# Rounding the weight slabs beside attention in quarters, between the units of the softmax

## The chip, the cores and the metric

The kernel runs on one core of one Trainium2 chip. The metric is the device time of one execution in microseconds; the median of three runs stands for a kernel. Besides TensorE (matmuls), a core has VectorE, ScalarE and GpSimd, each with its own instruction stream that is worked off in order, and SyncE, which here only starts DMAs. The engines meet through semaphores.

## What is computed

A decoder trunk of two layers over 272 positions (16 learned ones and 256 tokens) of width 1024, in float32. Layer 0 is sliding-window attention with 16 heads, 4 of keys and values, a sink for each head and a relative-position bias, followed by a dense SwiGLU. Layer 1 is RWKV-7 time mixing followed by a mixture of 8 experts, two for each token. After each of the four parts stands a layer norm of the weighted residual. The change lies beside attention:

```
qkv = einsum('bld,de->ble', x, w_qkv) + b_qkv
s_band = where(ok_band, q . k_band + bias_band, NEG_INF)      # and s_meta
m = max(max(s_band), max(s_meta), sink)
p_band = exp(s_band - m);  p_meta = exp(s_meta - m)
denom = sum(p_band) + sum(p_meta) + exp(sink - m)
o = (p_band . v_band + p_meta . v_meta) / denom
y = einsum('ble,ed->bld', o, w_o)
h = layer_norm(ALPHA * h + y)
```

## The kernel before

All large weights come as 395 slabs of 128x2048 float32 (1 MB). SyncE loads them in order into a ring of 7 slots, `ring`; from slab 7 on each load waits until the slab that had the slot has been split (`slab_taken`). A product is made from three: each operand is written as a rounded high half and a low half that is the rest, and high times high, high times low and low times high are added. For a slab, ScalarE writes the high half `w_hi` (`round_slab`, L1068 to L1073, the page's L1073), VectorE writes `w_lo` = `ring` - `w_hi` (`split_slab`, through the helper `tt` of L1364). Both have two buffers, slab n in n % 2. ScalarE may round slab n when the high half of slab n-2 has been used (`hi_free`) and slab n-2 has been split; VectorE may split it when slab n-2 has been multiplied (`slab_used`).

Slab 0 holds the key weights, 1 the values, 2 to 5 the queries (`SL_Q` = 2, two blocks of 128 queries each), 6 to 9 W_o (`SL_WO` = 6). The slabs that the change touches are 4, 5, 6 and 7.

Attention is cut into 24 units, a unit being one of three blocks of positions (96, 96 and 80 queries against 96, 192 and 224 keys) and two heads. They come in four periods of six, `s, r = divmod(u, 6)`; period s works on query blocks 2s and 2s+1, which slab 2+s gives. Each engine runs its own loop over u, written by hand:

- TensorE: `scores(u + 2)` (L611), which waits for the bias step of unit u+1; while s < 3 and r < 4 a fourth of the products of the next query slab (L593, L594, L599); `transposes(u - 1)` of the probabilities (L624); on even u the product of probabilities and values (L640).
- VectorE: waits for the exponentials of unit u, normalises it (L1447, L1449), then `biased(u + 2)`, which is the bias step (L1424, out of the PSUM banks of the scores, so that TensorE may write the next ones) and the minimum for the softmax (L1427); on even u the low half of an output block, `o_lo`; at r == 4 `split_slab(SL_Q + 2 + s)`.
- ScalarE: the exponentials of unit u+1 (L1121), the copy of the transposed probabilities of unit u-2 (L1138), on odd u the high half of an output block (L1129), at r == 3 the copy of the new queries (`keep_queries`, L1114), and at r == 4 `round_slab(SL_Q + 2 + s)`.

So at the fifth unit of every period one slab is rounded whole and split whole. Slabs 4 and 5 are multiplied in the next period, slabs 6 and 7 in the product with W_o behind the last unit. SyncE and GpSimd have nothing in the loop over units. Behind it come W_o, the layer norm, the dense layer and the rest, each on the result of the one before.

Of the kernel before, what the change touches and what calls it, by code (L numbers as in the profile page):

```python
# [20 lines left out]
F32, I32 = mybir.dt.float32, mybir.dt.int32  # L21
F32R = mybir.dt.float32r
ACT = mybir.ActivationFunctionType
# [17 lines left out]
SLOTS = 7  # L41
SL_K, SL_V, SL_Q, SL_WO = 0, 1, 2, 6
# [95 lines left out]
GROUP = 512  # L138
# [19 lines left out]
def build(nc, A, OUT):  # L158
    ctx = ExitStack()
    with ctx:  # L160
# [3 lines left out]
        def sem(name):  # L164
            return ctx.enter_context(nc.semaphore(name))

        ring = sb("ring", [P, SLOTS, TILES * P])
# [37 lines left out]
        to_head = carve(len(MASKS) * CH, KC, HEADS, memory=spare)  # L205
        from_head = carve(len(MASKS) * CH + KC * HEADS, KC, P, memory=spare)[0:HEADS]

        def columns_of(l):
            return slice(N_META if l == 3 else 0, T)

# [89 lines left out]
        w_hi = sb("w_hi", [P, 2, TILES * P], F32R)  # L300
        w_lo = sb("w_lo", [P, 2, TILES * P], F32R)
# [32 lines left out]
        loaded = [sem(f"slab_loaded{j}") for j in range(SLOTS)]  # L334


        hi_set, slab_taken = sem("slab_rounded"), sem("slab_split")
        hi_free, slab_used = sem("rounded_weights_used"), sem("slab_multiplied")
        h_hi_set, h_split = sem("h_rounded"), sem("h_split")
        dense_sig, dense_gate, gu_free = sem("dense_sigmoid"), sem("dense_gate"), sem("dense_hidden")  # L340
        dense_hi, dense_split = sem("dense_hidden_rounded"), sem("dense_hidden_split")
# [725 lines left out]
        def _(act):  # L1067
            def round_slab(n):  # L1068
                act.wait_ge(loaded[n % SLOTS], 16 * (n // SLOTS + 1))
                if n >= 2:  # L1070
                    act.wait_ge(hi_free, n - 1)
                    act.wait_ge(slab_taken, n - 1)
                act.activation(w_hi[:, n % 2, :], ring[:, n % SLOTS, :], ACT.Copy).then_inc(hi_set, 1)  # L1073

            def layer_norm(l):
                cols = columns_of(l)
                for k in range(KC):
                    act.wait_ge(ln_dve[l], k + 1)
                    act.activation(sq[:, k, cols], z[:, k, cols], ACT.Square).then_inc(ln_act[l], 1)
                act.wait_ge(ln_dve[l], 9)  # L1080
                act.activation(rstd[:, cols], rstd[:, cols], ACT.Sqrt).then_inc(ln_act[l], 1)
                for k in range(KC):
                    act.wait_ge(ln_dve[l], 11 + k)
                    act.activation(h[:, k, cols], z[:, k, cols], ACT.Identity, bias=v_of(f"b{l}", k))\  # L1084
                       .then_inc(ln_act[l], 1)
                    if l == 0:
                        act.activation(h_hi[:, k, :], z[:, k, :], ACT.Identity, bias=v_of(f"b{l}", k))\
                           .then_inc(h_hi_set, 1)
# [17 lines left out]
            for t in range(3):  # L1106
                n = min(P, T - P * t)
# [35 lines left out]
            for u in range(len(UNITS)):  # L1143
                s, r = divmod(u, 6)
                if u + 1 < len(UNITS):
                    exps(u + 1)
                if u >= 2:
                    keep_transposed(u - 2)
                if u >= 5 and u % 2:
                    keep_out((u - 5) // 2)  # L1150
                if s < 3 and r == 3:
                    keep_queries(s + 1)
                if r == 4:
                    round_slab(SL_Q + 2 + s)
            keep_transposed(len(UNITS) - 2)
            keep_transposed(len(UNITS) - 1)
            keep_out(len(UNITS) // 2 - 2)
# [41 lines left out]
            for j in range(12):  # L1199
                n = SL_RKV + j  # L1200
# [36 lines left out]
            for part, c, *level in order:  # L1237
                n, q = tokens_of(c), c % 2
# [110 lines left out]
        def _(dve):  # L1349
# [16 lines left out]
            def split_slab(n):  # L1366
                dve.wait_ge(hi_set, n + 1)
                if n >= 2:
                    dve.wait_ge(slab_used, n - 1)
                tt(w_lo[:, n % 2, :], ring[:, n % SLOTS, :], w_hi[:, n % 2, :].bitcast(F32), ALU.subtract)\  # L1370
                    .then_inc(slab_taken, 1)

            def left(lo, x, hi, wait, value, done):

                dve.wait_ge(wait, value)
                tt(lo, x, hi.bitcast(F32), ALU.subtract).then_inc(done, 1)
# [64 lines left out]
            for u, (t, m) in enumerate(UNITS):  # L1441
                s, r = divmod(u, 6)
                q0, qn, kn = Q_TILES[t]
                dve.wait_ge(sc_exp, u + 1)
                if u:
                    dve.wait_ge(sc_norm, u)
                nr.step(dve.reciprocal(rden[0:qn, :], den[0:qn, u % 4, :]))  # L1447
                for p in range(2):
                    i = dve.tensor_scalar(pr[0:qn, u % 4, p, 1:kn + 1], pr[0:qn, u % 4, p, 1:kn + 1],  # L1449
                                          rden[0:qn, p:p + 1], None, ALU.mult)  # L1450
                i.then_inc(sc_norm, 1)
                if u + 2 < len(UNITS):
                    biased(u + 2)
                if u >= 6 and u % 2 == 0:
                    split_out(u // 2 - 3)
                if r == 4:
                    split_slab(SL_Q + 2 + s)
            split_out(len(UNITS) // 2 - 3)
            split_out(len(UNITS) // 2 - 2)
            split_out(len(UNITS) // 2 - 1)  # L1460
# [24 lines left out]
            s = Steps(xx_steps)  # L1485
# [475 lines left out]
```

## Time and profile before

| | |
|---|---|
| median of 3 runs | 1764.15 us (1762.57 to 1768.33) |
| the profiled execution | 1763.99 us, of which the span of instructions is 1762.2 us |
| TensorE matmul busy | 1649.7 us (94%) |
| VectorE busy | 1295.3 us (74%) |
| ScalarE busy | 1000.0 us (57%) |
| the units of attention | about 38 to 121 us |
| mean granted TensorE clock | 0.955 of full speed |

The shares are means over stages with different limits. The experts take over half of the time; attention is 83 us of it. A timeline row gives start, duration, engine, line, operation, output and inputs, the count of merged instructions, and in brackets the idle time before it with what ended it. Instructions overlap a little at their ends, so the distance between two starts is the better price of an instruction in a row. In a row of windows the granted clock (PEclk) is 1.00 at the upper of TensorE's two levels, 2.4 GHz, and 0.50 at the lower, 1.2 GHz. The tile `arena` holds queries, scores and probabilities alike; its rows are told apart by their lines.

### The profile page before, as it was taken

The page shows a single profiled execution, that of the slowest core. Times are in us where ns is not written, and L with a number is a line of the kernel's source. Part 1 is how long each engine was busy: PE and PEld are TensorE (multiplying, and loading weights), DVE is VectorE, ACT ScalarE, POOL GpSimd, SP SyncE. Part 2 cuts the span into 40 slices and gives each one's busy share as a digit, 9 for nine tenths or more (in the row PEclk, how much of TensorE's full clock was granted, in tenths as well). Part 3 has the DMA queues.
Part 4 walks back from the last instruction along what each step waited for, and adds up shares of the span by engine and source line. Part 5 has one row for each costly group of instructions (what it writes and reads, how often), then busy time and mean ns, then how long its engine had stood idle before and what let it go on. Part 6 is the DMA issues. An engine that isn't in the chain of part 4 may idle for free.

```text
span 1762.2 us, 29867 instructions
## 1 busy us (share of the span) xinstructions
PE 1649.7 (94%) x12114; PEld 1297.7 (74%) x12114; DVE 1295.3 (74%) x1256; ACT 1000.0 (57%) x1027; POOL 72.8 (4%) x111
## 2 busy tenths in 40 slices
PE   7778999989999996799999999999999999999995
PEld 6557999967889974777777777777777777777774
DVE  3655554465755425579899899898998998998984
ACT  3544443334802212367777777777777777777773
POOL 3000000000035300000000000000000000000000
PEclk9869999989989986899999999999999999999997
DMA  9412544621400001249999999999999999999980
GB/s 262 169 49 102 183 168 167 226 101 51 166 26 4 4 3 48 103 150 374 368 358 371 372 354 372 369 358 370 359 369 372 357 369 370 359 371 366 361 330 26
DMA packets 60292, 425.42 MB, mean 241 GB/s; under 512 B 6887, under 2 KB 8023, under 8 KB 9224
## 3 DMA queue, kind: packets, MB, share of 16 engines
q1 hardware_dynamic: 58152, 416.52, 62.6%
q0 software_dynamic: 2016, 7.13, 1.6%
q8 instruction: 91, 1.49, 0.3%
q14 instruction: 33, 0.27, 0.0%
HBM read 422.28 MB, written 1.12 MB: 240 GB/s over the span
## 4 chain that ended last, share of the span: by engine, by line
PE 71%; DVE 3%; ACT 2%; issue 1%; ACTq 0%; POOL 0%; DVEq 0%
PE PS L512 53%; PE PS L798 6%; PE PS L513 5%; PE PS L1012 1%; PE PS L814 1%; DVE arena L1364 1%; PE PS L968 1%; PE PS L823 1%; PE PS L552 1%; PE PS L998 0%; PE PS L999 0%; PE PS L558 0%; PE PS L936 0%; PE PS L776 0%; ACT h L1084 0%
## 5 line engine op out<-in xcount | busy, mean ns | idle before, releaser
L1364 DVE TENSOR_TENSOR w_lo<-ring,w_hi 128x2048 fp32r<-128x2048 f32 x395 | 903.3, 2288 | 208.9 <-ACT w_hi L1293 88.5
L1293 ACT ACTIVATE w_hi<-ring 128x2048 fp32r<-128x2048 f32 x336 | 644.7, 1919 | 264.3 <-PE PS L512 241.7
L512 PE MATMUL PS<-w_hi,x_hi 128*96 128x512 f32 x896 | 353.9, 395 | 0.7 <-ACT x_hi L1285 0.7
L512 PE MATMUL PS<-w_hi,x_lo 128*96 128x512 f32 x896 | 352.5, 393 | 0.0
L512 PE MATMUL PS<-w_lo,x_hi 128*96 128x512 f32 x896 | 243.0, 392 | 0.0
L1073 ACT ACTIVATE w_hi<-ring 128x2048 fp32r<-128x2048 f32 x59 | 112.9, 1914 | 168.2 <-issue 89.3
L512 PEld LDWEIGHTS PS<-w_lo,x_hi 128*96 128x96 f32 x896 | 144.6, 161 | 62.1
L512 PEld LDWEIGHTS PS<-w_hi,x_lo 128*96 128x96 f32 x896 | 144.8, 162 | 58.2
L512 PEld LDWEIGHTS PS<-w_hi,x_hi 128*96 128x96 f32 x896 | 144.6, 161 | 58.1 <-ACT x_hi L1285 1.0
L512 PE MATMUL PS<-w_hi,hid_hi 128*96 128x512 f32 x448 | 176.7, 394 | 0.0
L512 PE MATMUL PS<-w_hi,hid_lo 128*96 128x512 f32 x448 | 176.0, 393 | 0.0
L512 PE MATMUL PS<-w_lo,hid_hi 128*96 128x512 f32 x448 | 121.9, 394 | 0.0
L798 PE MATMUL PS<-arena 64*64 64x64 f32 (+6 forms) x3360 | 110.9, 218 | 5.6 <-DVE arena L1364 2.3
L798 PEld LDWEIGHTS PS<-arena 64*64 64x64 f32 (+3 forms) x3360 | 102.3, 131 | 13.8 <-issue 9.6
L1258 ACT ACTIVATE arena<-PS 128x256 f32<-128x256 f32 (+2 forms) x84 | 32.3, 389 | 141.2 <-PE PS L798 88.0
L1364 DVE TENSOR_TENSOR arena<-arena,PS 128x272 f32<-128x272 f32 (+6 forms) x102 | 54.4, 535 | 60.2 <-PE PS L798 56.5
L513 PE MATMUL PS<-h_hi,w_hi 128*128 128x272 f32 x352 | 91.2, 293 | 6.8 <-DVE h_lo L1364 6.7
L512 PEld LDWEIGHTS PS<-w_lo,hid_hi 128*96 128x96 f32 x448 | 72.2, 161 | 31.7
L512 PEld LDWEIGHTS PS<-w_hi,hid_hi 128*96 128x96 f32 x448 | 72.2, 161 | 30.8
L512 PEld LDWEIGHTS PS<-w_hi,hid_lo 128*96 128x96 f32 x448 | 72.3, 161 | 30.7
L513 PE MATMUL PS<-h_lo,w_hi 128*128 128x272 f32 x352 | 90.7, 291 | 0.0
L1364 DVE TENSOR_TENSOR experts<-experts,PS 96x512 f32<-96x512 f32 (+1 forms) x113 | 76.0, 672 | 0.0
(258 smaller groups left out, 2035.8 us busy)
## 6 DMA issues: line engine op xcount, KB each, us to landing
ring<-in_slabs SPq DMA_DIRECT2D x395, 1024.0 KB, 4.9
arena<-in_lora POOLq DMA_DIRECT2D x1, 1152.0 KB, 5.4
h<-in_h SPq DMA_DIRECT2D x1, 1088.0 KB, 6.6
arena<-bias_lines POOLq DMA_DIRECT2D x1, 1056.0 KB, 19.9
arena<-bias_lines POOLq DMA_DIRECT2D x1, 1040.0 KB, 24.6
arena<-in_lora POOLq DMA_DIRECT2D x1, 1024.0 KB, 12.0
out<-h SPq DMA_DIRECT2D x1, 1024.0 KB, 4.7
arena<-in_lora POOLq DMA_DIRECT2D x1, 512.0 KB, 6.5
```

Source lines behind the costliest of these rows:

```text
L512: return pe.matmul(out, x, w, start=start, stop=stop) if tokens_stay else \
L513: pe.matmul(out, w, x, start=start, stop=stop)
L552: mm = pe.matmul(PS[:, 0, cols], ones_d[:, :], z[:, k, cols], start=k == 0, stop=k == KC - 1)
L798: mm = pe.matmul(PS[64 * p:64 * p + n_out, b + g, at:at + width], lhsT(m, p), rhs(m, p), start=i == 0, stop=i == len(pairs) - 1)
L814: mm = pe.matmul(out[64 * p:64 * p + n, :, 0:n], by_feature(x, c)(m, p), r_kk[64 * p:64 * p + 64, :, T * m + CH * c:T * m + CH * c + n], s ...
L823: mm = pe.matmul(PS[64 * p:64 * p + n, b + g, col + CH * (m % 4):col + CH * (m % 4 + 1)], x(m, p), masks[64 * p:64 * p + 64, MASKS.index(" ...
L968: mm = pe.matmul(PS[:, 2 * (j % 4) + i, 0:HALF], rows[:, t, P * k:P * k + P], pick[:, t, 4 * half:4 * half + 4, :].rearrange("p e c -> p ( ...
L1012: mm = pe.transpose(PS[:, 4 + g % 2, CAP * j:CAP * (j + 1)], hid_rows[0:CAP, g % 2, P * j:P * (j + 1)], eye[0:CAP, 0:CAP])
L1073: act.activation(w_hi[:, n % 2, :], ring[:, n % SLOTS, :], ACT.Copy).then_inc(hi_set, 1)
L1258: act.activation(out, rows, ACT.Copy).then_inc(c_act, 1)
L1293: act.activation(w_hi[:, n % 2, :], ring[:, n % SLOTS, :], ACT.Copy).then_inc(hi_set, 1)
L1364: tt = lambda o, a, b, op=ALU.mult: dve.tensor_tensor(out=o, in0=a, in1=b, op=op)
```

## The change

The rounding and the split of slabs 4 to 7 are each done in four parts of 512 columns. ScalarE does quarter r behind its work of unit r of the period, r = 0 to 3, instead of the whole at r = 4. VectorE does quarter r - 1 behind its work of unit r, r = 1 to 4. The conditions that the whole rounding waited for stand before quarter 0 (and are asked for four units earlier), the one of the split before VectorE's quarter 0. Two new semaphores count the first three quarters; the last quarter of each kind counts `hi_set` and `slab_taken` as the whole did, so TensorE's and SyncE's conditions are unchanged. `GROUP` is 512.

```diff
+        def quarter(x, i):
+            return x[:, GROUP * i:GROUP * (i + 1)]
...
+        part_hi, part_lo = sem("slab_quarters_rounded"), sem("slab_quarters_split")
...
+            def round_quarter(n, i):
+                if i == 0:
+                    act.wait_ge(loaded[n % SLOTS], 16 * (n // SLOTS + 1))
+                    act.wait_ge(hi_free, n - 1)
+                    act.wait_ge(slab_taken, n - 1)
+                act.activation(quarter(w_hi[:, n % 2, :], i), quarter(ring[:, n % SLOTS, :], i), ACT.Copy)\
+                   .then_inc(hi_set if i == 3 else part_hi, 1)
...
                 if s < 3 and r == 3:
                     keep_queries(s + 1)
-                if r == 4:
-                    round_slab(SL_Q + 2 + s)
+                if r < 4:
+                    round_quarter(SL_Q + 2 + s, r)
...
+            def split_quarter(n, i):
+                if i == 3:
+                    dve.wait_ge(hi_set, n + 1)
+                else:
+                    dve.wait_ge(part_hi, 3 * (n - SL_Q - 2) + i + 1)
+                if i == 0:
+                    dve.wait_ge(slab_used, n - 1)
+                tt(quarter(w_lo[:, n % 2, :], i), quarter(ring[:, n % SLOTS, :], i),
+                   quarter(w_hi[:, n % 2, :].bitcast(F32), i), ALU.subtract)\
+                    .then_inc(slab_taken if i == 3 else part_lo, 1)
...
-                if r == 4:
-                    split_slab(SL_Q + 2 + s)
+                if 1 <= r < 5:
+                    split_quarter(SL_Q + 2 + s, r - 1)
```

The first place is VectorE in the second period, from the minimum of unit 11 over the bias step of unit 12 to that of unit 13 (both L1424, 96x2x97). Before:

```order
L1427 TENSOR_REDUCE arena<-arena 80x2
L1447 RECIPROCAL arena<-arena 80x2
L1449 TENSOR_SCALAR arena<-arena 80x224 x2
L1424 SCALAR_TENSOR_TENSOR arena<-PS,arena 96x2x97
L1427 TENSOR_REDUCE arena<-arena 96x2
L1364 TENSOR_TENSOR o_lo<-PS,o_hi 128x2x80
L1364 TENSOR_TENSOR w_lo<-ring,w_hi 128x2048
L1447 RECIPROCAL arena<-arena 80x2
L1449 TENSOR_SCALAR arena<-arena 80x224 x2
L1424 SCALAR_TENSOR_TENSOR arena<-PS,arena 96x2x97
```

The same stretch of VectorE in the changed kernel, whose lines are 12 to 23 higher:

```order
L1450 TENSOR_REDUCE arena<-arena 80x2
L1376 TENSOR_TENSOR w_lo<-ring,w_hi 128x512
L1470 RECIPROCAL arena<-arena 80x2
L1472 TENSOR_SCALAR arena<-arena 80x224 x2
L1447 SCALAR_TENSOR_TENSOR arena<-PS,arena 96x2x97
L1450 TENSOR_REDUCE arena<-arena 96x2
L1376 TENSOR_TENSOR o_lo<-PS,o_hi 128x2x80
L1376 TENSOR_TENSOR w_lo<-ring,w_hi 128x512
L1470 RECIPROCAL arena<-arena 80x2
L1472 TENSOR_SCALAR arena<-arena 80x224 x2
L1447 SCALAR_TENSOR_TENSOR arena<-PS,arena 96x2x97
```

The whole w_lo ahead of the bias step of unit 13 has become one of 128x512; another of them now stands ahead of the bias step of unit 12, and two more before this piece.

The second place is ScalarE at the turn from unit 9 to unit 10: the copies of the queries (L1114), the exponentials of unit 11 (L1121, 80x225), the transposed probabilities (L1138), and then, before:

```order
L1129 ACTIVATE o_hi<-PS 128x2x80
L1114 ACTIVATE arena<-PS,vec 128x272 x2
L1121 ACTIVATE arena<-arena 80x225 x2
L1138 ACTIVATE arena<-PS 128x2x96
L1138 ACTIVATE arena<-PS 64x2x96
L1073 ACTIVATE w_hi<-ring 128x2048
L1121 ACTIVATE arena<-arena 96x97 x2
```

And the same stretch of ScalarE in the changed kernel:

```order
L1141 ACTIVATE o_hi<-PS 128x2x80
L1126 ACTIVATE arena<-PS,vec 128x272 x2
L1084 ACTIVATE w_hi<-ring 128x512
L1133 ACTIVATE arena<-arena 80x225 x2
L1150 ACTIVATE arena<-PS 128x2x96
L1150 ACTIVATE arena<-PS 64x2x96
L1133 ACTIVATE arena<-arena 96x97 x2
```

The fourth quarter of w_hi stands behind the queries and ahead of the exponentials of unit 11; nothing stands any more between the transposed probabilities and the exponentials of unit 12.

## Rows read from the trace of the kernel before

**Rows 1.** TensorE's waits, 36 to 122 us: total us, times, longest us.

```profile
PE PS L611 <- DVE arena L1424: 14.6, 6, 4.4
```

**Rows 2.** Busy us by window, with TensorE's granted clock (PEclk).

```profile
core 0: us, PE busy (x) PEld busy (x) DVE busy (x) ACT busy (x) POOL busy (x), PEclk, DMA share, GB/s
40.00:42.00 2.00, 1.46 (x7) 0.96 (x7) 1.61 (x6) 1.55 (x8) 0.00 (x0) 0.64 1.01 188
...
78.00:80.00 2.00, 0.02 (x2) 0.05 (x2) 1.93 (x6) 0.00 (x0) 0.00 (x0) 0.52 0.00 0
...
108.00:110.00 2.00, 2.00 (x13) 0.94 (x10) 1.42 (x6) 1.44 (x6) 0.00 (x0) 0.50 0.02 4
...
124.00:126.00 2.00, 2.00 (x11) 2.00 (x10) 0.00 (x0) 0.00 (x0) 0.00 (x0) 0.53 0.00 0
```

**Rows 3.** Timeline of VectorE, bias step of unit 12 to that of unit 13.

```profile
73.92 0.36 DVE L1424 SCALAR_TENSOR_TENSOR arena<-PS,arena 96x194 f32<-96x194 f32 x1 [1.11 <-PE PS L611]
...
74.58 0.31 DVE L1364 TENSOR_TENSOR o_lo<-PS,o_hi 128x160 fp32r<-128x160 f32 x1
76.59 2.29 DVE L1364 TENSOR_TENSOR w_lo<-ring,w_hi 128x2048 fp32r<-128x2048 f32 x1 [1.70 <-ACT w_hi L1073]
78.80 0.15 DVE L1447 RECIPROCAL arena<-arena 80x2 f32<-80x2 f32 x1
...
79.49 0.35 DVE L1424 SCALAR_TENSOR_TENSOR arena<-PS,arena 96x194 f32<-96x194 f32 x1
```

**Rows 4.** Timeline of ScalarE at 74.65 us.

```profile
74.65 1.91 ACT L1073 ACTIVATE w_hi<-ring 128x2048 fp32r<-128x2048 f32 x1
```

**Rows 5.** Timeline of TensorE, the score products (L611) of four units.

```profile
67.09 0.61 PE L611 MATMUL PS<-arena 64*80 64x225 f32 x4
...
70.19 0.61 PE L611 MATMUL PS<-arena 64*80 64x225 f32 x4
...
79.98 0.96 PE L611 MATMUL PS<-arena 64*96 64x193 f32 x4 [4.38 <-DVE arena L1424]
...
85.59 0.57 PE L611 MATMUL PS<-arena 64*96 64x193 f32 x4
```

**Rows 6.** Timeline of VectorE, the bias steps (L1424) of units 10 and 11.

```profile
67.75 0.62 DVE L1424 SCALAR_TENSOR_TENSOR arena<-PS,arena 80x450 f32<-80x450 f32 x1 [0.60 <-PE PS L611]
...
70.85 0.62 DVE L1424 SCALAR_TENSOR_TENSOR arena<-PS,arena 80x450 f32<-80x450 f32 x1 [0.91 <-PE PS L611]
```

**Rows 7.** Groups by form, 0 to 700 us: count, busy us, mean ns, idle.

```profile
L1073 ACT ACTIVATE w_hi<-ring 128x2048 fp32r<-128x2048 f32 x57 | 109.1, 1914 | 159.7 <-issue 89.3 <-PE PS L513 68.9 <-DMA ring<-in_slabs 1.5
...
L1258 ACT ACTIVATE arena<-PS 128x512 f32<-128x512 f32 x8 | 4.8, 597 | 51.1 <-PE PS L823 51.1
...
L1364 DVE TENSOR_TENSOR w_lo<-ring,w_hi 128x2048 fp32r<-128x2048 f32 x57 | 130.6, 2291 | 119.9 <-ACT w_hi L1073 88.4 <-PE PS L513 23.4 <-PE PS L512 8.0
...
L1364 DVE TENSOR_TENSOR arena<-arena 128x504 f32<-128x504 f32 x4 | 2.5, 676 | 0.0
```

**Rows 8.** Timeline of VectorE, the split of slab 4 and of slab 6.

```profile
55.46 2.29 DVE L1364 TENSOR_TENSOR w_lo<-ring,w_hi 128x2048 fp32r<-128x2048 f32 x1 [1.93 <-ACT w_hi L1073]
...
97.45 2.29 DVE L1364 TENSOR_TENSOR w_lo<-ring,w_hi 128x2048 fp32r<-128x2048 f32 x1 [1.70 <-ACT w_hi L1073]
```

**Rows 9.** Timeline of VectorE and TensorE in the last six units.

```profile
105.14 0.56 DVE L1424 SCALAR_TENSOR_TENSOR arena<-PS,arena 96x386 f32<-96x386 f32 x1 [1.34 <-PE PS L611]
...
109.66 0.62 DVE L1424 SCALAR_TENSOR_TENSOR arena<-PS,arena 80x450 f32<-80x450 f32 x1 [0.54 <-PE PS L611]
...
114.27 2.29 DVE L1364 TENSOR_TENSOR w_lo<-ring,w_hi 128x2048 fp32r<-128x2048 f32 x1 [2.42 <-ACT w_hi L1073]
...
117.30 0.80 PE L624 MATMUL PS<-eye,arena 80*128 80x80 f32 x4 [3.96 <-DVE arena L1449]
```

**Rows 10.** The ring of slabs, 0 to 42 us: DMA issues and landings.

```profile
L403 SPq DMA_DIRECT2D ring<-in_slabs x6: 426/466/672, 2.0 to 4.7; - x6
...
DMA to landing us min/median/max: 9.6/14.6/27.4
```

## The prediction

> **What bounds the kernel now.** I read the page first (one core, span 1762.2 us, the program itself 1763.99 us), then the waits of TensorE over the attention units, then the timelines of VectorE, ScalarE and TensorE over one period of six units, then the busy time in small windows with the granted clock. What follows attention hangs on its output: the product with W_o, both norms, RWKV and the experts come one after the other, each with its own slabs, so a microsecond taken out of attention should leave the end earlier by one.
>
> In attention the reader should see a period of about 21 us with one hole in it. TensorE waits for the bias step of VectorE (L1424) 6 times, 14.6 us in all, the longest 4.4 us [rows 1]. The hole behind unit 13 reads so on VectorE: after the bias step of unit 12 at 73.92 and the low half of an output at 74.58 it stands idle 1.70 us for ScalarE's w_hi, spends from 76.59 to 78.80 on w_lo, and only then normalises unit 11 and reaches the bias step of unit 13 at 79.49 [rows 3]. ScalarE began that w_hi at 74.65 [rows 4]. TensorE's next score products wait for that bias step, 4.38 us, until 79.98 [rows 5]. The same hole stands behind slab 4 (1.93 us of waiting) and slab 6 (1.70) [rows 8], and behind slab 7 (2.42), after which the last transposes wait 3.96 us [rows 9].
>
> The second cost is the clock. In the window 78 to 80 us, behind the idle stretch, the granted clock is 0.52 on average, that is, it has fallen from the upper level (2.4 GHz) to the lower (1.2 GHz) [rows 2]. From one score product to the next with twelve query products between them it takes 3.10 us at the upper level (67.09 to 70.19) and 5.61 us behind the hole (79.98 to 85.59) [rows 5].
>
> **What a quarter costs.** Nothing of 512 elements from SBUF to SBUF in this type stands in the trace, so I take the neighbours [rows 7]. VectorE: a subtraction of 128x504 takes 676 ns and one of 128x2048 2291 ns, so the quarter takes 0.68; the whole one lasts 2.29 but its follower starts after 2.21 (76.59 to 78.80 [rows 3]), and with the same 0.08 of overlap a quarter holds the engine 0.61 us. The bounds are 0.55 (a fourth of 2.21) and 0.69 (no overlap). ScalarE: 128x512 out of PSUM takes 597 ns, 128x2048 out of SBUF 1914; I take 0.55 us, between 0.48 (a fourth) and 0.60. Four quarters are then 2.44 us on VectorE where 2.21 stood, and 2.2 on ScalarE where 1.9 stood.
>
> **Where the quarters lie.** The first three VectorE quarters of a slab come after the bias steps of units 3, 4, 5 of a period, counted from the one with the first quarter. VectorE idles there before its next bias step, waiting for score products: 0.60 us, 0.91 us [rows 6] and 1.11 us [rows 3]. Quarters of 0.61 fit, the first one to within 0.01 us. At the bound of 0.69 the first would be 0.09 late, which the next idle of 0.91 takes back. The ScalarE quarters 0 to 2 go ahead of exponentials which wait for VectorE anyway. The fourth ScalarE quarter stands after the queries are kept and in front of the exponentials of unit 11, and makes them 0.55 us later; they then end at about 74.8, and the normalisation that needs them is held by the fourth quarter on VectorE until 75.5. It costs nothing while that holds. The first quarter also asks for its slab four units earlier, slab 4 at about 41.6 us: the six first slabs are issued by 4.7 us and the slowest lands 27.4 us after its issue, so by 32.1 [rows 10], and slab 4 is there. Nothing is passed on SyncE or GpSimd; the slab counts as split at the same place in VectorE's order as before, a little earlier in time, and a ring slot refilled earlier helps nobody here.
>
> **What the hole gives back.** At the unit where the whole split stood, VectorE now has one quarter whose rounded part is long there. The wait for w_hi goes, and 2.21 becomes 0.61, 1.60 less. Slab 4: 1.93 + 1.60 = 3.53. Slab 5: 1.70 + 1.60 = 3.30. Slab 6: 3.30. Together **10.13 us** [rows 3, 8]. The next late thing is VectorE still: unit 13's bias step moves from 79.49 to about 76.2, and TensorE keeps a wait of about 1.0 us (4.38 less 3.30) in place of 4.38.
>
> Slab 7 lies beside six units with no query products, in which VectorE is nearly full: it idles 1.34 us before the bias step at 105.14 and 0.54 before that at 109.66 [rows 9]. The hole gives 2.42 + 1.60 = 4.02. The three quarters placed before it cost 3 x 0.61 = 1.83, of which the idle of 0.54 takes its part; the 1.34 lies ahead of the first quarter and hides nothing. That leaves 4.02 - 1.83 + 0.54 = **2.73 us**. If TensorE is at the upper clock when these six units begin, the 1.34 us of waiting for it goes too, and the term is **4.07 us**.
>
> **What the clock gives back.** Behind the two holes that are followed by query products (slabs 4 and 5) the first unit would run at the upper level. It has eight products with values of 192 columns rather than 160 and four transposes rather than two, so I allow 3.3 us rather than 3.10: 5.61 - 3.3 = 2.3, twice **4.6 us** [rows 5]; the other start is taken to be like this one. The reason to think that the clock holds: it fell where TensorE had stood idle over 3 us, and the remaining wait is 1.0 us. The reason against: between 40 and 42 us the mean clock is 0.64 although TensorE's matmuls cover 1.46 of the 2 us [rows 2], so it has also fallen in work with small holes, the units before the first query products.
>
> The Trainium skill has both sides, on the page "TensorE: Matmul & The Clock Gate": the section "HAM oscillation — how this bites in real kernels" says that an idle stretch between groups of matmuls puts the clock back, so that each group starts slow, and "A second HAM failure mode: psum-queue depth-cycling" says that frequent small holes can do it too. By the first rule the sum is the forecast below; by the second it is the first rival.
>
> **The sum.** 10.13 + 4.07 + 4.6 = 18.8 us. The profiled execution took 1763.99, and the median of the three runs is 1764.15, so the two are one to within 0.2: 1763.99 - 18.8 = **1745.2 us**. Later stages have clock falls of their own, and moving them in time can shift each a little either way; I allow 2 us for it.
>
> **Rivals.**
> - The small holes are enough: the clock still falls at each end of a period. Then only the waits go: 10.13 + 2.73 = 12.9, **1751.1 us**. For it: the window at 40 us. Against it: here dense query products run until just before, and the hole is a fourth as long.
> - The clock holds to the end: it is low from before 100 us to 125.9 now (0.50 in 108 to 110, 0.53 in 124 to 126 [rows 2]), and from the last transposes at 117.30 [rows 9] to 125.9 there are 8.6 us of nearly dense work. At the upper level half of it goes, 4.3 us more: **1740.9 us**. Against it: the last six units keep TensorE thinly used, as at 40 us.
> - The hole is not VectorE's but someone's behind it: with the split gone from unit 11 the transposed probabilities or the exponentials end last at the same time. Then nothing is gained, **1764 us**. Against it: ScalarE is done with unit 12's exponentials before VectorE asks for them, and L1424 waits for nothing else.
> - Slower: the clock falls in the small holes and does not rise again, as it stays at 0.50 in 108 to 110 us though TensorE's matmuls cover the whole 2.00 us [rows 2]. Each unit with query products then costs 5.61 instead of 3.3, 2.3 us more. There are nine such units at the upper level now (three in each of three periods). The balance turns after 12.9 / 2.3 = 5.6 units; with all nine it is 20.7 - 12.9 = 7.8 us more, **1771.8 us**. Against it: in each period the query products, run together, have brought the clock back up.
>
> **How the numbers follow.** The forecast has 0.50, the clock that falls as before 0.25, the clock that holds to the end 0.17, no gain 0.05, slower 0.03. A measurement of this kernel can tell about 0.3%, 5.3 us. The first three are faster by over that, together 0.92; no gain is within it, 0.05; slower 0.03. The range takes in the first three with the 2 us of the later stages partly on each side, 1739 to 1753. The quarter bounds move the sum by little: at 0.69 on VectorE each of three holes gives 0.08 less and slab 7 four times that, 0.6 in all.
>
> **What would show it.** On VectorE, w_lo of 128x512, 16 of them of about 0.68 us, and on ScalarE 16 of w_hi of about 0.6, and hardly any idle for w_hi before them. TensorE's waits for L1424 in attention down from 14.6 to some 4 us. A first unit of a period of 3.3 us with the clock at 1.00 if the forecast is right, of 5.6 us at 0.50 if the first rival is. The end of attention at about 102 us where it was 121. Wrong would be: quarters that cost VectorE over 0.9 us, so that the idle of 0.60 and 0.91 no longer hides them, or TensorE waiting for ScalarE's transposed probabilities.

## The result and the profile after

The changed kernel takes 1748.33 us, the median of 6 runs (1745.1 to 1751.17), beside 1763.86 us of the kernel before (1762.3 to 1768.33); the ratio is 0.9911, with a 95% interval of 0.9894 to 0.9927. That is 15.5 us less; 1745.2 was forecast, within 1739 to 1753. A second set of 6 runs has 1749.43 us beside 1762.47, 13.0 less. The profiled execution took 1745.1 us, 18.9 less than the one of before (1763.99). That it comes so near to the sum of 18.8 is chance, as is shown below.

The waits of TensorE on the bias step, over the same window as [rows 1] (L1447 is now what L1424 was, L615 the score products that were L611):

```profile
PE PS L615 <- DVE arena L1447: 3.3, 6, 0.7
```

14.6 us have become 3.3, and the longest wait 0.7 in place of 4.4. VectorE in the timeline of the second period, to be read against [rows 3, 6]:

```profile
66.91 0.62 DVE L1447 SCALAR_TENSOR_TENSOR arena<-PS,arena 80x450 f32<-80x450 f32 x1 [0.31 <-PE PS L615]
...
69.98 0.35 DVE L1447 SCALAR_TENSOR_TENSOR arena<-PS,arena 96x194 f32<-96x194 f32 x1 [0.51 <-PE PS L615]
...
70.64 0.31 DVE L1376 TENSOR_TENSOR o_lo<-PS,o_hi 128x160 fp32r<-128x160 f32 x1
70.88 0.68 DVE L1376 TENSOR_TENSOR w_lo<-ring,w_hi 128x512 fp32r<-128x512 f32 x1
71.47 0.15 DVE L1470 RECIPROCAL arena<-arena 80x2 f32<-80x2 f32 x1
...
72.16 0.35 DVE L1447 SCALAR_TENSOR_TENSOR arena<-PS,arena 96x194 f32<-96x194 f32 x1
```

The row at 70.88 is the last quarter of w_lo. It begins where the low half of the output ends, with no wait for w_hi, and unit 13's bias step comes 2.18 us after unit 12's (69.98 to 72.16), where 5.57 us stood. The idle stretches ahead of the bias steps of units 11 and 12 are 0.31 and 0.51 us, and were 0.91 and 1.11: each quarter took 0.60 us out of an idle stretch and nothing else. The first quarter uses up the 0.60 us ahead of unit 10, whose bias step (63.81) now waits for nothing. The groups by form give what one quarter lasts on VectorE and on ScalarE:

```profile
L1376 DVE TENSOR_TENSOR w_lo<-ring,w_hi 128x512 fp32r<-128x512 f32 x16 | 10.8, 677 | 0.0
```

```profile
L1084 ACT ACTIVATE w_hi<-ring 128x512 fp32r<-128x512 f32 x16 | 9.9, 621 | 0.0
```

TensorE's score products in the same period, the counterpart of [rows 5], with the one row of transposes (L628) that has a wait between them:

```profile
63.15 0.61 PE L615 MATMUL PS<-arena 64*80 64x225 f32 x4
...
66.25 0.61 PE L615 MATMUL PS<-arena 64*80 64x225 f32 x4
...
71.48 0.47 PE L628 MATMUL PS<-eye,arena 80*128 80x80 f32 x4 [0.25 <-ACT arena L1150]
...
72.66 0.68 PE L615 MATMUL PS<-arena 64*96 64x193 f32 x4 [0.70 <-DVE arena L1447]
...
77.59 0.57 PE L615 MATMUL PS<-arena 64*96 64x193 f32 x4
```

The wait is 0.70 us where it was 4.38. A middle unit takes 3.10 us as before (63.15 to 66.25). But the first unit of the next period, 72.66 to 77.59, takes 4.93 us, and not the 3.3 that were forecast. The windows say why:

```profile
core 0: us, PE busy (x) PEld busy (x) DVE busy (x) ACT busy (x) POOL busy (x), PEclk, DMA share, GB/s
72.00:74.00 2.00, 1.34 (x7) 1.02 (x8) 1.90 (x8) 1.77 (x10) 0.00 (x0) 0.75 0.44 127
74.00:76.00 2.00, 2.00 (x11) 2.00 (x10) 1.29 (x5) 1.53 (x6) 0.00 (x0) 0.50 0.94 397
76.00:78.00 2.00, 2.00 (x18) 1.18 (x17) 0.00 (x0) 0.78 (x4) 0.00 (x0) 0.90 0.00 0
88.00:90.00 2.00, 1.04 (x11) 0.65 (x9) 1.90 (x9) 1.77 (x9) 0.00 (x0) 1.00 0.25 41
90.00:92.00 2.00, 2.00 (x13) 1.02 (x12) 1.93 (x8) 2.00 (x10) 0.00 (x0) 0.51 0.88 365
...
110.00:112.00 2.00, 2.00 (x16) 2.00 (x16) 0.00 (x0) 0.00 (x0) 0.00 (x0) 0.87 0.00 0
```

The granted clock is 0.75 on average from 72 to 74, 0.50 from 74 to 76 and 0.90 from 76 to 78. It still falls to the lower level; it falls inside the first unit instead of ahead of it. In the last period it falls at about 90 us and stays down until after 110.

The table goes through all traces by stage, in us, as starts of TensorE's instructions show it; the experiments that its rows name follow below. "Attention" runs from the first score products to the very last transpose, "last period" from the score products that open the last six units to that transpose, "W_o" from it to the last low product of W_o, "down" from the first high product (the one that reads `w_hi`) to the first low one (which reads `w_lo`) of the dense down projection, "recurrence" from the first to the last product of L798, and "norm to out" from the first product of the group norm (L783) to RWKV's first output product.

| kernel | median (runs) | attention | last period | W_o | down | recurrence | norm to out |
|---|---|---|---|---|---|---|---|
| before | 1763.86 (6) | 79.2 | 17.0 | 29.3 | 6.7 | 143.5 | 17.8 |
| changed | 1748.33 (6) | 63.7 | 13.5 | 29.2 | 4.1 | 142.7 | 17.8 |
| after_again | 1749.43 (6) | 63.5 | 13.2 | 29.4 | 6.6 | 142.6 | 20.2 |
| act_quarters | 1757.42 (1) | 72.7 | 14.4 | 29.5 | 6.6 | 142.0 | 17.8 |
| last_slab | 1760.35 (1) | 76.5 | 14.0 | 29.2 | 6.6 | 141.6 | 17.6 |
| whole_moved | 1745.67 (4) | 60.5 | 13.9 | 28.6 | 5.6 | 146.9 | 17.3 |
| fill | 1745.52 (4) | 60.6 | 12.1 | 29.1 | 4.1 | 147.1 | 17.3 |
| fill_dn | 1750.05 (6) | 63.7 | 13.5 | 29.1 | 4.1 | 145.4 | 20.2 |
| moved_fill3 | 1747.77 (5) | 62.2 | 15.7 | 25.8 | 5.4 | 147.1 | 17.5 |
| moved_fill_all | 1743.75 (5) | 62.2 | 15.7 | 25.8 | 4.1 | 143.1 | 17.8 |
| mixed | 1743.35 (5) | 58.5 | 12.2 | 28.6 | 5.7 | 140.8 | 17.7 |
| mixed_fill | 1740.79 (4) | 58.6 | 12.2 | 25.8 | 4.1 | 147.0 | 17.4 |

The long stages do not move: from the first scatter of an expert to the last it is 844.9 to 845.0 us in every one of the twelve traces.

### The profile page after: what moved, and what is told of

Its sections match the earlier page's. It is cut to its first block, busy times and chain, and to the rows that moved or that the text cites. A ratio compares the mean times of both kernels' runs of the same rounds, so it can differ in the third digit from the quotient of the medians.

```text
span 1743.3 us, 29891 instructions
## 1 busy us (share of the span) xinstructions
PE 1644.6 (94%) x12114; PEld 1294.1 (74%) x12114; DVE 1295.1 (74%) x1268; ACT 1001.1 (57%) x1039; POOL 72.7 (4%) x111
## 4 chain that ended last, share of the span: by engine, by line
PE 72%; DVE 3%; ACT 2%; issue 1%; ACTq 0%; POOL 0%; DVEq 0%
PE PS L516 53%; PE PS L802 6%; PE PS L517 5%; PE PS L1016 1%; PE PS L818 1%; DVE arena L1376 1%; PE PS L972 1%; PE PS L827 1%; PE PS L556 1%; PE PS L1002 0%; PE PS L1003 0%; PE PS L562 0%; PE PS L940 0%; PE PS L780 0%; ACT h L1096 0%
## 5 line engine op out<-in xcount | busy, mean ns | idle before, releaser
L1376 DVE TENSOR_TENSOR w_lo<-ring,w_hi 128x2048 fp32r<-128x2048 f32 (+1 forms) x407 | 904.9, 2225 | 199.3 <-ACT w_hi L1077 89.9
L1305 ACT ACTIVATE w_hi<-ring 128x2048 fp32r<-128x2048 f32 x336 | 644.7, 1919 | 264.2 <-PE PS L516 241.4
L1077 ACT ACTIVATE w_hi<-ring 128x2048 fp32r<-128x2048 f32 x55 | 105.3, 1915 | 166.1 <-issue 89.0
L802 PEld LDWEIGHTS PS<-arena 64*64 64x64 f32 (+3 forms) x3360 | 102.4, 132 | 13.2 <-issue 8.5
L516 PEld LDWEIGHTS PS<-w_hi,hid_lo 128*96 128x96 f32 x448 | 72.3, 161 | 30.6
```

Source lines behind the costliest of these rows:

```text
L516: return pe.matmul(out, x, w, start=start, stop=stop) if tokens_stay else \
L802: mm = pe.matmul(PS[64 * p:64 * p + n_out, b + g, at:at + width], lhsT(m, p), rhs(m, p), start=i == 0, stop=i == len(pairs) - 1)
L1376: tt = lambda o, a, b, op=ALU.mult: dve.tensor_tensor(out=o, in0=a, in1=b, op=op)
```

## The experiments

**Only ScalarE in quarters.** The rounding in quarters, the split whole at the fifth unit.

```diff
-                if 1 <= r < 5:
-                    split_quarter(SL_Q + 2 + s, r - 1)
+                if r == 4:
+                    split_slab(SL_Q + 2 + s)
```

> ScalarE rounds slabs 4 to 7 in quarters as in the changed kernel, but VectorE splits each whole at the fifth unit, as before. The stretch from the first score products to the last transposes is 78.7 us before and 63.3 us in the changed kernel. If my account of the hole holds (the wait for w_hi and the length of the split count one for one), only the waits go: 1.93 + 1.70 + 1.70 + 2.42 = 7.75 us, so a stretch of about 71 us, and TensorE still waits about 2.7 us for each of the bias steps behind a hole. If the wait alone is what matters and the split is covered by other work once it can start early, the stretch is near 63 us. If the quarters on ScalarE cost as much as they give (by delaying the exponentials), it is near 78.

Measured 1757.42 us in one run. The stretch is 72.3 us (to the group of the last transposes, as the expectation counts; the table counts to the last one), near the 71 of the first reading and far from 63 and 78, so the other two readings are out. Three score products of this trace, the first with its wait:

```profile
75.89 0.96 PE L615 MATMUL PS<-arena 64*96 64x193 f32 x4 [2.31 <-DVE arena L1447]
...
82.01 0.96 PE L615 MATMUL PS<-arena 64*96 64x193 f32 x4
...
85.94 0.61 PE L615 MATMUL PS<-arena 64*80 64x225 f32 x4
```

The wait behind a hole is 2.31 us where it was 4.38 and where the fully quartered kernel has 0.70, so each of the two parts, the wait for w_hi and the length of the split, counts by itself (2.7 us of waiting were expected to be left). What is missing against 71 is the clock's: the first unit here takes 6.12 us (75.89 to 82.01) and the second 3.93, together 2.1 more than the 5.61 and 2.36 of the kernel before. The reading rests on the trace, since one run says little of a median.

**Only the slab beside the last period.**

```diff
-                if r < 4:
+                if s == 3 and r < 4:
                     round_quarter(SL_Q + 2 + s, r)
+                if s < 3 and r == 4:
+                    round_slab(SL_Q + 2 + s)
```

and the same on VectorE.

> Only slab 7, beside the last six units, is done in quarters; slabs 4, 5 and 6 are whole at the fifth unit as before. By the sum, with the lower clock in these six units, 2.7 us: from the score products that open the last period to the last transposes 16.46 us before, 13.7 here (the changed kernel shows 13.0). If the quarters' 1.83 us in a nearly full VectorE eat the gain, 15.5 or more.

Measured 1760.35 us in one run. The last period in its trace:

```profile
101.04 0.96 PE L615 MATMUL PS<-arena 64*96 64x193 f32 x4 [4.38 <-DVE arena L1449]
...
114.51 0.80 PE L628 MATMUL PS<-eye,arena 80*128 80x80 f32 x4 [0.46 <-DVE arena L1474]
```

101.04 to 114.51 is 13.47 us, 2.99 less than the 16.46 of before; 2.73 was the term at the lower clock. The quarters in a nearly full VectorE cost about what the term says. This is the last period with quarters at the lower clock throughout, which the table shows as 14.0 us.

**The whole slabs at another place.** No quarters at all: ScalarE rounds in the first unit, VectorE splits in the second, ahead of the bias step.

```diff
-                if r < 4:
-                    round_quarter(SL_Q + 2 + s, r)
+                if r == 0:
+                    round_slab(SL_Q + 2 + s)
...
+                if r == 1:
+                    split_slab(SL_Q + 2 + s)
                 if u + 2 < len(UNITS):
                     biased(u + 2)
...
-                if 1 <= r < 5:
-                    split_quarter(SL_Q + 2 + s, r - 1)
```

> Each of the slabs 4 to 7 is rounded whole by ScalarE in the first unit of its period and split whole by VectorE in the second, between the normalisation and the bias step, where VectorE idles 2.7 to 2.9 us in the changed kernel behind the query products of a first unit. If what matters is where the work lies and not that it is cut up, the split is hidden there: nothing of it is left in the fifth unit, 0.6 us less in each of three periods than with quarters, and about 1.4 less in the last one (2.44 us of quarters against 2.21 whole, less an idle stretch of 1.2 us): a stretch from first score products to last transposes of about 60 us and a time of 1745. If small pieces are needed, because a whole split delays the bias step of the second unit and TensorE with it, it is over 63.3 us and the time above 1748.

Measured 1745.67 us (1742.1 to 1749.09), ratio 0.9894 (0.9867 to 0.9921). The attention is 60.5 us in the table, 3.2 less than with quarters. VectorE in its third period, TensorE's score products and a window beside them:

```profile
72.15 0.44 DVE L1472 TENSOR_SCALAR arena<-arena 96x96 f32<-96x96 f32 x2
73.24 2.29 DVE L1376 TENSOR_TENSOR w_lo<-ring,w_hi 128x2048 fp32r<-128x2048 f32 x1 [0.65 <-ACT w_hi L1077]
75.45 0.55 DVE L1447 SCALAR_TENSOR_TENSOR arena<-PS,arena 96x386 f32<-96x386 f32 x1
```

```profile
69.93 0.57 PE L615 MATMUL PS<-arena 64*96 64x193 f32 x4 [0.39 <-DVE arena L1447]
...
73.36 0.57 PE L615 MATMUL PS<-arena 64*96 64x193 f32 x4
```

```profile
72.00:74.00 2.00, 2.00 (x19) 1.09 (x18) 1.32 (x5) 2.00 (x6) 0.00 (x0) 1.00 0.00 0
```

The whole w_lo at 73.24 lies where VectorE waited for score products, and the bias step follows at 75.45. TensorE's wait is 0.39 us, the first unit takes 3.43 us (69.93 to 73.36) and the clock is 1.00. So in the first three periods cutting the work up was not what helped, but taking it out of the fifth unit: they take 46.6 us in place of 50.3. Of these 3.7 us, 3.0 are the clock's, in the two first units (4.96 and 4.93 us with quarters, 3.43 each here).

The last period went otherwise than expected: 13.9 us, not less than the 13.5 with quarters, although 1.4 less was said. Its wait at the third unit is 1.48 us, since there are no query products to cover a whole split. But it also runs at another clock: its opening score products take 0.96 us, the lower level, where those of the changed kernel take 0.57.

```profile
84.00:86.00 2.00, 1.61 (x13) 0.88 (x11) 1.74 (x8) 1.90 (x11) 0.00 (x0) 0.74 0.00 0
```

```profile
85.06 0.96 PE L615 MATMUL PS<-arena 64*96 64x193 f32 x4 [0.39 <-DVE arena L1447]
...
91.27 1.04 PE L615 MATMUL PS<-arena 64*80 64x225 f32 x4 [1.48 <-DVE arena L1447]
```

Like for like, at the lower clock throughout, the whole slab (13.9) and the quarters (14.0 in the kernel before this one) cost the last period the same. The clock fell here behind a wait of 0.39 us, the same wait behind which it held in this trace one period earlier.

**Extra matmuls in the small holes.** The changed kernel, with matmuls of 256 columns in the sixth unit.

```diff
+            def fill(n):
+                for _ in range(n):
+                    pe.matmul(PS[:, 6, 0:256], sq_r[:, 0, 0:P], sq_r[:, 1, 0:256], start=True, stop=True)
...
                     queries(s + 1, r)
+                if s < 3 and r == 5:
+                    fill(3)
...
                     probs_times_values(u // 2 - 2)
+                if s < 3 and r == 5:
+                    fill(8)
```

> The changed kernel with 11 extra matmuls of 256 columns in the sixth unit of each of the first three periods, into a PSUM bank that is free there, in the small waits of TensorE; their results are not used. If the small holes are what lets the clock fall, the granted clock stays at the upper level in the first unit of the next period and this unit (score products to score products) takes 3.3 us in place of 4.96 and 4.93: 3.3 us less in all, about 1745. If the clock falls for another reason (few columns in the fifth and sixth unit as a whole), the two units stay near 4.9 us and the time at 1748 or slightly above.

Measured 1745.52 us (1743.56 to 1747.34), ratio 0.9896 (0.9874 to 0.9918). The first unit of the second period, and a window inside it:

```profile
56.55 0.57 PE L615 MATMUL PS<-arena 64*96 64x193 f32 x4
...
59.98 0.57 PE L615 MATMUL PS<-arena 64*96 64x193 f32 x4
```

```profile
56.00:58.00 2.00, 2.00 (x17) 1.61 (x16) 1.55 (x6) 1.99 (x9) 0.00 (x0) 1.00 0.86 270
```

It takes 3.43 us at a granted clock of 1.00, where the changed kernel has 4.96; the one of the third period takes 3.43 too. The attention falls from 63.7 to 60.6 us. The 3.3 us of the expectation are nearly met, but not as it says: the two first units give 3.0, the sixth units, longer by the extra matmuls, take 1.2 back, and the last period, which now begins its second unit at the upper clock too, gives 1.4. In the changed kernel the sixth unit has holes of 0.25 and 0.47 to 0.70 us, and the clock falls at the end of each of the first three periods in all three traces of it (with the one that adds matmuls ahead of the down projection); with the extra matmuls, in one trace, it does not. They shorten the holes and add columns at once, so whether it is the holes or the thin use of TensorE in the fifth and sixth unit that loses the clock is not told apart.

**The changed kernel again, and its spread.**

> The changed kernel once more, for its spread beside the others. The profiled execution of it was 1745.1 us with a median of 1748.3 and a range of 6 us. If the spread comes from the clock in later stages, this trace shows the same attention (63.3 us from the first score products to the last transposes, within 0.5) and differs from the first one after it: the start of the dense down projection took 4.1 us from its first high product to its first low one there (upper clock), and 6.7 in the kernel before (lower clock). If the spread is attention's own, the 63.3 us change by 1 to 3 us.

Measured 1749.43 us (1745.27 to 1753.37). The attention is the same within 0.2 us. The span of this trace is 1751.6 us, 8.3 more than that of the first: 1.3 before the first score products, 2.5 at the down projection, 2.4 between the recurrence and the output products, and the rest in small pieces elsewhere. The spread is not attention's. The place at the down projection as the traces of before and of the changed kernel have it (count, shortest, median and longest, first and last start):

```profile
L513 PE MATMUL PS<-dh_hi,w_hi x176: 283/288/596, 301.1 to 367.5; 128*128 128x272 f32 x176
...
L513 PE MATMUL PS<-dh_hi,w_lo x176: 282/288/293, 307.8 to 369.7; 128*128 128x272 f32 x176
```

```profile
L517 PE MATMUL PS<-dh_hi,w_hi x176: 283/288/392, 286.0 to 349.9; 128*128 128x272 f32 x176
...
L517 PE MATMUL PS<-dh_hi,w_lo x176: 282/288/293, 290.1 to 352.0; 128*128 128x272 f32 x176
```

From 301.1 to 307.8 there are 6.7 us, from 286.0 to 290.1 there are 4.1, over the same products.

**Extra matmuls ahead of the down projection.**

```diff
+            for _ in range(28):
+                pe.matmul(PS[:, 6, 0:256], h_hi[:, 0, 0:P], h_hi[:, 1, 0:256], start=True, stop=True)
             pe.wait_ge(gu_free, FT + 2)
```

> The changed kernel with 28 extra matmuls of 256 columns in the wait of 3.5 us ahead of the dense down projection, their results unused. If the granted clock at that point is what moved between the profiles, the first high to the first low product of the down projection takes 4.1 us in this trace, the median is 1 to 2.6 us under that of the changed kernel run beside it, and the spread is smaller. If the spread comes from elsewhere (the recurrence, the norms), median and spread are as without it, or up to 0.5 us longer.

Measured 1750.05 us (1747.36 to 1754.21) beside 1749.43. The place takes 4.1 us in this trace, but the median and the spread are as without it. The down projection is one place of several, and the others are larger: the recurrence took between 140.8 and 147.1 us over the twelve traces with no change in it. The longer ones go with a lower granted clock near their end: from 600 to 620 and from 620 to 640 us it is 0.82 and 0.59 in the trace with 147.1 (`fill`), and 1.00 and 0.74 in the one with 140.8 (`mixed`). Whether the 28 matmuls give anything on average is not settled; the kernel without them has 4.1 in one of its two traces as well.

**Whole slabs moved and the last period filled, alone and with the down projection.**

```diff
+                if s == 3:
+                    fill({0: 4, 1: 8, 2: 6, 3: 8, 4: 6, 5: 12}[r])
```

> The kernel with whole slabs moved to the first and second unit, and 44 extra matmuls of 256 columns spread over the last six units, where TensorE waits. In the trace without them the clock is at the lower level from about 85 us to 105.3. If it is the thin use of TensorE in the last period that loses the clock, it now stays up into the product with W_o: the last period loses about 1 us (1.3 of VectorE's waiting at its start) and the dense work behind it some 4, so a time 4 to 5 us under that of the moved kernel (1745.7), near 1741. If the extra matmuls come too late or delay the score products, the last period grows (12.9 us from its score products to the last transposes) and nothing is gained.

> Both of the additions together: whole slabs moved, the last six units filled, and the 28 matmuls ahead of the dense down projection. If the terms add, about 1739 to 1740 us, the fastest of these kernels; if the clock at the down projection does not matter, as the kernel without them, near 1741.

Measured 1747.77 us (1746.49 to 1748.84) and 1743.75 us (1740.42 to 1745.63). The expectations gave the moved kernel's last period as 12.9 us; that counts to the start of a group of eight transposes, and to the last of them, as in the table, it is 13.9. Both traces agree up to the dense layer: W_o takes 25.8 us where it took 28.6, since the clock is up when it begins, but the last period takes 15.7 us where the moved kernel has 13.9, and the attention with W_o is 88.0 us beside 89.1. All of the growth lies behind the third score products of the last period, where 32 of the 44 extra matmuls stand: up to there both kernels take 6.2 us from the opening ones, from there to the last transpose 9.5 in place of 7.7. The clock did not stay up all the time either; behind the wait of the third unit it fell, and it came back before W_o (rows of the second kernel):

```profile
92.14 0.61 PE L615 MATMUL PS<-arena 64*80 64x225 f32 x4 [1.83 <-DVE arena L1455]
```

```profile
94.00:96.00 2.00, 2.00 (x10) 1.22 (x9) 1.30 (x5) 1.44 (x6) 0.00 (x0) 0.50 0.90 381
...
98.00:100.00 2.00, 2.00 (x21) 1.58 (x19) 1.48 (x6) 1.61 (x8) 0.00 (x0) 1.00 0.00 0
```

The expectation of 1741 for the first was missed, and so was the one of 1739 to 1740 for the second. The two medians differ by 4.0 us where the matmuls ahead of the down projection could give 1.3 (5.4 to 4.1), and the two recurrences by 4.0 in their traces; medians of five runs are not better than this spread.

**Quarters only where no query products are.** Slabs 4 to 6 moved whole, slab 7 in quarters.

```diff
+                if s < 3 and r == 0:
+                    round_slab(SL_Q + 2 + s)
+                if s == 3 and r < 4:
+                    round_quarter(SL_Q + 2 + s, r)
```

and on VectorE the split whole in the second unit for s < 3, quarters for s == 3.

> Slabs 4, 5 and 6 moved whole (rounded in the first, split in the second unit of the period, where VectorE waits for query products), slab 7 in quarters, since the last period has no query products and its second unit no such wait. If a whole split is free only where the query products cover it, the first three periods are as in the moved kernel (46.6 us from the first score products to those that open the last period) and the last one shorter than its 12.9 us: with the moved kernel's start at the upper clock, 11.7 to 12.5 us. If the quarters cost the last period what the whole split does, it stays at 12.9.

Measured 1743.35 us (1742.23 to 1746.49), ratio 0.9903 (0.9885 to 0.992). The last period takes 11.7 us to the start of its last group of transposes (86.10 to 97.83), 12.2 to the last one where the moved kernel has 13.9, and the attention 58.5: the shorter end of what was expected. Part of this is the clock's, which the expectation left out of its rival: here the last period begins at the upper level, with the same code ahead of it as in the moved kernel, where it began at the lower.

```profile
86.10 0.57 PE L615 MATMUL PS<-arena 64*96 64x193 f32 x4 [0.40 <-DVE arena L1449]
...
91.76 0.61 PE L615 MATMUL PS<-arena 64*80 64x225 f32 x4 [0.77 <-DVE arena L1449]
...
93.84 0.55 PE L628 MATMUL PS<-eye,arena 96*128 96x96 f32 x4 [0.99 <-DVE arena L1474]
```

```profile
92.00:94.00 2.00, 1.01 (x10) 0.50 (x7) 1.97 (x7) 1.70 (x7) 0.00 (x0) 1.00 0.03 8
94.00:96.00 2.00, 1.15 (x8) 0.39 (x7) 1.93 (x6) 1.26 (x6) 0.00 (x0) 0.61 0.00 0
```

At the lower clock the two ways cost the same, as said above. At the upper one they differ in the first two units: from the opening score products to the third ones it is 3.3 us here, with quarters, and 6.2 in the two moved and filled kernels, which also begin at the upper level, and 6.2 in the moved one at the lower level too; with a whole slab VectorE waits for the whole w_hi there and then takes 2.3 us for the split. The quarters cost more behind that point (8.9 us to the last transpose beside 7.7 in the moved kernel). So the 1.7 us are won by the quarters and the upper clock together; no trace has the whole split at the upper clock without extra matmuls.

> The mixed kernel with 28 extra matmuls of 256 columns in the waits of the last six units, fewer than the 44 of before, and 28 ahead of the dense down projection. With 44 the clock stayed up into W_o and gave 3.4 us there, but the last period grew from 12.9 to 15.5 us. If that growth came from the whole split and the fill together, and 28 leave the score products alone, the last period takes under 12.5 us and W_o from its first to its last low product stays at 25.8 us after the last transposes in place of 28.6: some 4 us under the moved and filled kernel (1743.8), near 1740. If the clock falls with so few extra matmuls, W_o takes 28.6 and the time is that of the mixed kernel.

Measured 1740.79 us (1739.42 to 1742.65), ratio 0.9882 (0.9862 to 0.9901), the lowest median of these kernels and 2.6 us under the mixed one beside it, though its interval overlaps those of the mixed, the moved and the filled ones; the changed kernel has 0.9911 and 0.9923. Its edit is `fill({0: 0, 1: 6, 2: 3, 3: 6, 4: 3, 5: 10}[r])` in the last period and the 28 matmuls of above. Windows of its trace at the end of attention and in W_o:

```profile
94.00:96.00 2.00, 1.17 (x9) 0.62 (x7) 1.93 (x7) 1.26 (x7) 0.00 (x0) 1.00 0.00 0
...
98.00:100.00 2.00, 2.00 (x22) 1.12 (x20) 0.34 (x1) 0.82 (x4) 0.00 (x0) 1.00 0.91 279
...
102.00:104.00 2.00, 2.00 (x19) 2.00 (x18) 0.00 (x0) 0.00 (x0) 0.00 (x0) 1.00 0.00 0
```

The clock stays at 1.00 through the thin stretch at 94 to 96 and into W_o. The last period keeps its length (58.6 us of attention beside 58.5), and W_o takes 25.8 us beside 28.6. So the growth of the last period in the two moved and filled kernels does not come with every fill. Two things differ here, the quarters in place of the whole split and 28 extra matmuls in place of 44, and which of them mattered is not told apart.

## Why the prediction was right, and where not

**The hole.** Right, and in size. From the period's second score products to the next period's first, before and after: 15.25 and 11.87 us for slab 5 (3.38 less; 3.30 was said), 15.25 and 11.86 for slab 6 (3.39; 3.30); for slab 4, from the first score products, 20.29 and 16.63 (3.66; 3.53). Together 10.4 us beside 10.13. The wait that TensorE keeps is 0.70 us (0.47 behind the first period), where about 1.0 was said, and the waits for the bias step are 3.3 us in all, where some 4 were. That both parts of a term (the wait and the difference in length) count one for one is shown by the kernel with quarters on ScalarE alone, which has only the first.

**The price of a quarter and its cover.** Right: 677 ns on VectorE (0.68), 621 on ScalarE (0.60 was the upper bound there, so it was slightly over; the fourth one is hidden behind VectorE as said). The bound of 0.69 was not needed.

**The last period.** 3.45 us (16.46 to 13.01), between the 2.73 and the 4.07 of the two clocks. The rows show both at work:

```profile
89.45 0.57 PE L615 MATMUL PS<-arena 64*96 64x193 f32 x4 [0.70 <-DVE arena L1447]
...
92.30 0.96 PE L615 MATMUL PS<-arena 64*96 64x193 f32 x4
...
102.46 0.80 PE L628 MATMUL PS<-eye,arena 80*128 80x80 f32 x4 [0.45 <-DVE arena L1472]
```

The score products at 89.45 take 0.57 us, the upper level, those at 92.30 0.96, the lower. With the clock held until about 97 us (the kernel with filled sixth units) the period took 11.65 us, 4.81 less than before; with the clock lost from its start (last slab only) 2.99 less. Both ends of this term were put a little low, by 0.74 and 0.26 us.

**The clock.** Here the forecast failed in size: 2 x 2.3 us were said, and 0.92 + 0.68 = 1.6 came (5.88 to 4.96 and 5.61 to 4.93). The step that failed is the reason given for it, that the clock had fallen where TensorE stood idle over 3 us and that the remaining wait was 1.0 us. The row against it stood in the prediction, the window 40 to 42 at 0.64 with small holes, and it was the better guide: the sixth unit has holes of 0.25 and 0.70 us, and the clock falls inside the unit behind it. The first rival had the clock right, but not quite its price: the fall comes later than behind a hole of 4.38 us, inside the first unit, which gives 1.6 us that it did not count. The Trainium skill tells of this on the page "TensorE: Matmul & The Clock Gate", in "A second HAM failure mode: psum-queue depth-cycling": frequent small idle stretches between groups of matmuls make the clock fall and rise again. By that, the traces agree in the main: the first unit takes 4.93 us behind the holes, and 3.43 where they are filled or shortened to 0.4. So what the fall costs is shown; what brings it about is not, since with such a shortened hole of 0.39 us the clock fell as well, at one of fifteen ends of a period (the moved kernel at 85).

**The sum.** 10.4 + 1.6 + 3.45 = 15.5 us in attention, and 15.5 us in the medians (13.0 in the second set of runs). The forecast was 3.1 us under the measured median and the first rival 2.8 us over it, so the time alone does not choose between them; the range held because it takes in both. The first rival's 12.9 with the 1.6 and half of the last period's 1.34 would have been 15.1. The forecast of 18.8 met the profiled execution to 0.1 us only because in that one the down projection began at the upper clock and in the one of before at the lower, 2.6 us; the rest of the 3.4 us outside attention is in small changes of the recurrence and the starting time. The prediction allowed 2 us for such things; the twelve runs of the changed kernel lie between 1745.1 and 1753.4, which is more like 4 to each side. W_o begins at 106.1 us where it began at 121.0; about 102 was said.

**The other rivals.** That the clock holds into W_o did not happen (29.2 us after 29.3), though it can be had: 25.8 us when the last period is filled. No gain and slower did not happen; the clock did come back in each period of query products.

## What to carry to other kernels

Work that two engines hand to each other in one piece stops a tight loop for the sum of both lengths; move it to where its engine already waits. Where no such wait is long enough, pieces that fit the small waits can do better: here they did in a period at the upper clock, and cost the same at the lower. Small waits of TensorE can cost more than their length, by the clock of the dense products behind them, and a few matmuls whose results nobody reads can keep it, if they do not themselves delay the loop. Compare traces stage by stage before believing that a sum was met, and look at the clock of a stage before giving its length to the code: two executions of one kernel differed by 8 us here in stages that nothing had touched, and one unchanged place began at the upper clock in four traces and at the lower in a fifth.

## What was not expected of the hardware

- How long a wait loses the clock has no one answer in these traces. Behind waits of 0.25 and 0.70 us in a unit of 1.8 us it fell at each of nine ends of a period in three traces (0.50 in the window 74 to 76). With one of 0.39 to 0.42 us in their place it held at fourteen of fifteen ends, in five traces, and fell at the fifteenth (0.74 in 84 to 86 of the moved kernel). In the last period of the mixed kernel it was still at 1.00 from 92 to 94, behind a wait of 0.77 us and with one of 0.99 inside that window.
- The same program's recurrence took 140.8 to 147.1 us in twelve traces, and the stretch behind it 17.3 to 20.2 us, while the experts took 845.0 in all.
